# A mixture-of-experts stage in float32: the one-hot gather and combine as two rounded passes, with the routing weights moved to the silu product

## The chip, the cores and the metric

The program runs on one NeuronCore of a Trainium2 chip. The metric is device time in microseconds (us) of one execution. Engines are named as in the profile: PE (TensorE matmul) and PEld (its weight loads), DVE (VectorE), ACT (ScalarE), POOL (GpSimd), and SP, whose queue issues the weight DMAs.

## The reference, cut to what matters

256 tokens of width 1024 pass two blocks. The first has two layers of a mixer, a layer norm, a mixture of experts and a layer norm; the second has dense feed-forward layers and another mixer. The change touches the mixture of experts alone, once in each of the two layers of the first block:

```python
grp_logits = xf @ w_grp + b_grp               # 4 groups, the best one is taken
exp_logits = xf @ w_exp + b_exp               # 8 experts in a group, the best 2 are taken
gate = p_grp[:, None] * softmax(top_l)        # weight of each of a token's 2 experts
...
hdn = silu(xb @ w_gate[e]) * (xb @ w_up[e])   # xb: the tokens of expert e
y = hdn @ w_down[e]
out = zeros.at[tok].add(y * gate_weight)
```

There are 32 experts, each with three float32 matrices of 2 MB (1024 by 512 twice, 512 by 1024 once), so 201 MB are read for each layer. All inputs and outputs are float32.

## The kernel before, in words

**Work.** Experts are taken in 16 pairs of two (`N_PAIRS`); each expert has 64 places (`CAP`), so a pair fills 128 columns. `route_dve` leaves in `k.rank` the place of each token at each expert and in `k.gate_w` its weight. For pair g:

- `select_dve` compares `k.rank` with the numbers 0 to 63 (L1203) into the 0/1 matrix `sel` (two blocks of 128 tokens by 128 places), and multiplies it by `gate_w` (L1212) into `sel_w`.
- `gather_pe` gathers the pair's tokens as a product: for each of 8 slices kk of the width and each of 2 token blocks one float32 matmul with `x_tok[:, tb, kk::8]` as the stationary operand, that is 128 columns whose elements lie 8 words apart, and `sel` as the moving one, 128 wide. It then transposes `sel_w` (L1228). `gather_act` (L1237, L1241) and `gather_dve` (L1249) copy the results out of PSUM to `xg` and `sel_wT`.
- `paired_pe` (L1262) multiplies by gate, up and down: the two experts of the pair use 64 columns of the array each, 512 wide, 16 float32 products for each of the three matrices.
- ACT takes silu (L1326), DVE multiplies by up (L1350) into `h`; PE transposes `h` (L1309), ACT copies it out as `hT` (L1332) for down.
- ACT (L1336) and DVE (L1358) each copy one half of the result `y` out of PSUM. `combine_pe` multiplies the transposed weighted selection by `y`, four float32 products 512 wide, and `combine_dve` adds them to `acc` (L1289).

A line of PE is often that of a helper: L225 is `mm`, which issues the gather, the combine and all projections; the operands tell them apart (gather: `arena,x_tok` 128x128; combine: `arena` 128x512).

**Order.** Each engine runs a list written out by hand. On PE, for pair g: gate(g), up(g), gather(g+1), transposes of h(g), combine(g-1), down(g). After the last pair comes its combine. PSUM has 8 banks of 512 float32; gate uses bank 0, up bank 1, down banks 2 and 3, and all else takes banks 4 to 7 in turn (`B_BANKS`); `Banks.open` waits until the bank's former contents were read.

**Weights.** `Ring` gives each 1 MB chunk of weights a slot. In the expert stages there are 12 slots, which is one pair; SP loads a chunk of pair g+1 when the product that reads the chunk of pair g in its slot has ended (`loads_sp`, L355).

**Rounded operands.** Elsewhere the kernel splits a float32 operand in a rounded high part (float32r, ACT copy, L414) and a low part, the rest (DVE subtract, L421), and sums three rounded products. L1390 is the down product of the dense layers: 4 of them, 22 tiles each, 4 output banks, three products each, 512 wide. `x_tok` is kept in float32; its transposed parts `xT_high` and `xT_low` serve the router and lie idle while the experts run. L449 transposes `x_tok` with the same spaced columns.

Of the kernel before, what the change touches and what calls it, by code (L numbers as in the profile page):

```python
# [6 lines left out]
F32 = mybir.dt.float32  # L7
# [7 lines left out]
P = 128  # L15
# [30 lines left out]
PAIR = 2  # L46
BIG = 1e30
# [1129 lines left out]
def expert_tiles(k):  # L1177
    A = k.arena
    A.restart()
    b = Tiles()  # L1180
    b.sel = [A.take(NB, P) for _ in range(2)]
    b.sel_w = [A.take(NB, P) for _ in range(2)]
    b.sel_wT = [A.take(T) for _ in range(3)]
    b.xg = [A.take(KT, P) for _ in range(2)]
    b.silu, b.h, b.hT = A.take(BANK), A.take(BANK), A.take(FT_E, P)
    b.y = [A.take(D) for _ in range(2)]
    b.spill = [flat(k.mixT[:, :, :]), k.pool_or_distance[:, :]]
    return b


def two_experts(v):
    return v.rearrange("p (a b) -> p a b", a=PAIR)


def select_dve(e, k, X, g):
    S, b, i = X.S, k.experts, g % 2
    e0 = slice(PAIR * g, PAIR * g + PAIR)
    if g >= 2:
        e.wait_ge(*S.product[X.key("gather", g - 2)])
    if g == 0 and X.main:  # L1200
        e.wait_ge(*S.route_step["rank", X.layer])
    for tb in range(NB):
        ins = e.tensor_tensor(two_experts(b.sel[i][:, tb, :]), mid_bcast(k.tab("slot_no"), PAIR), bcast(k.rank[:, tb, e0], CAP), ALU.is_equal)  # L1203
    ins.then_inc(*S.selected.tell(X.key("slots", g)))
    if g == 0 and X.main:
        weigh_dve(e, k, X.layer)
        e.wait_ge(*S.route_step["weights", X.layer])
    e.wait_ge(*S.selected[X.key("slots", g)])
    if g >= 2:
        e.wait_ge(*S.product[X.key("turned_weights", g - 2)])  # L1210
    for tb in range(NB):
        ins = e.tensor_tensor(two_experts(b.sel_w[i][:, tb, :]), two_experts(b.sel[i][:, tb, :]), bcast(k.gate_w[:, tb, e0], CAP), ALU.mult)  # L1212
    ins.then_inc(*S.selected.tell(X.key("weights", g)))


def gather_pe(e, k, X, g):
    S, b, i = X.S, k.experts, g % 2
    for half in range(2):
        view = pairs(X.banks.open(e, B_BANKS, X.key("xg", g, half))[:, :], 4)
        if half == 0:  # L1220
            e.wait_ge(*S.selected[X.key("slots", g)])
        for kk in range(4):
            ins = mm(e, view[:, kk, :], [(k.x_tok[:, tb, (4 * half + kk)::KT], b.sel[i][:, tb, :]) for tb in range(NB)])
        ins.then_inc(*S.product.tell(X.key("gather", g) if half else X.key("gather", g, 0)))
    bank = X.banks.open(e, B_BANKS, X.key("sel_wT", g))
    e.wait_ge(*S.selected[X.key("weights", g)])
    for tb in range(NB):
        ins = e.transpose(bank[:, block(tb)], b.sel_w[i][:, tb, :], k.ident)  # L1228
    ins.then_inc(*S.product.tell(X.key("turned_weights", g)))


def gather_act(e, k, X, g):
    S, b = X.S, k.experts
    if g >= 2:
        e.wait_ge(*S.expert[X.key("up", g - 2, 1)])
    e.wait_ge(*S.product[X.key("gather", g, 0)])
    e.activation(b.xg[g % 2][:, 0:4, :], pairs(X.banks[X.key("xg", g, 0)][:, :], 4), ACT.Copy).then_inc(*S.act_out.tell(X.key("xg", g, 0)))  # L1237
    if g >= 3:
        e.wait_ge(*S.product[X.key("combine", g - 3, 1, 1)])
    e.wait_ge(*S.product[X.key("turned_weights", g)])  # L1240
    e.activation(b.sel_wT[g % 3], X.banks[X.key("sel_wT", g)][:, 0:T], ACT.Copy).then_inc(*S.act_out.tell(X.key("sel_wT", g)))  # L1241


def gather_dve(e, k, X, g):
    S, b = X.S, k.experts
    if g >= 2:
        e.wait_ge(*S.expert[X.key("up", g - 2, 1)])
    e.wait_ge(*S.product[X.key("gather", g)])
    e.tensor_copy(b.xg[g % 2][:, 4:8, :], pairs(X.banks[X.key("xg", g, 1)][:, :], 4)).then_inc(*S.dve_out.tell(X.key("xg", g, 1)))  # L1249
# [17 lines left out]
def combine_pe(e, k, X, g):  # L1267
    S, b, i = X.S, k.experts, g % 2
    for tb in range(NB):
        for n in range(2):  # L1270
            bank = X.banks.open(e, B_BANKS, X.key("add", g, tb, n))
            if tb == 0 and n == 0:
                e.wait_ge(*S.act_out[X.key("sel_wT", g)])
                e.wait_ge(*S.act_out[X.key("y", g, 0)])
                e.wait_ge(*S.dve_out[X.key("y", g, 1)])
            mm(e, bank[:, :], [(b.sel_wT[g % 3][:, block(tb)], b.y[i][:, BANK * n:BANK * n + BANK])]).then_inc(*S.product.tell(X.key("combine", g, tb, n)))
# [15 lines left out]

def experts_pe(e, k, X):
    S, b = X.S, k.experts
    gather_pe(e, k, X, 0)
    for g in range(N_PAIRS):
        i = g % 2
        gate = X.banks.open(e, (0,), X.key("silu", g))
        e.wait_ge(*S.act_out[X.key("xg", g, 0)])
        e.wait_ge(*S.dve_out[X.key("xg", g, 1)])  # L1300
        paired_pe(e, k, X, [gate], "gate", g, KT // 2, b.xg[i])
        up = X.banks.open(e, (1,), X.key("h", g))
        paired_pe(e, k, X, [up], "up", g, KT // 2, b.xg[i])
        if g + 1 < N_PAIRS:
            gather_pe(e, k, X, g + 1)
# [10 lines left out]
    combine_pe(e, k, X, N_PAIRS - 1)  # L1316


def experts_act(e, k, X):
    S, b = X.S, k.experts  # L1320
    gather_act(e, k, X, 0)
    for g in range(N_PAIRS):
# [4 lines left out]
        if g + 1 < N_PAIRS:  # L1327
            gather_act(e, k, X, g + 1)
# [4 lines left out]
        if g >= 2:  # L1333
            e.wait_ge(*S.product[X.key("combine", g - 2, 1, 1)])
        e.wait_ge(*S.expert[X.key("down", g, 1)])
        e.activation(b.y[g % 2][:, 0:BANK], X.banks[X.key("y", g, 0)][:, :], ACT.Copy).then_inc(*S.act_out.tell(X.key("y", g, 0)))  # L1336


def experts_dve(e, k, X):
    S, b = X.S, k.experts  # L1340
    select_dve(e, k, X, 0)
    gather_dve(e, k, X, 0)
    for g in range(N_PAIRS):
        if g + 1 < N_PAIRS:
# [3 lines left out]
        e.wait_ge(*S.act_out[X.key("silu", g)])
        e.wait_ge(*S.expert[X.key("up", g, 1)])
        e.tensor_tensor(b.h, b.silu, X.banks[X.key("h", g)][:, :], ALU.mult).then_inc(*S.dve_out.tell(X.key("h", g)))  # L1350
        if g + 1 < N_PAIRS:
            gather_dve(e, k, X, g + 1)
        if g:
            combine_dve(e, k, X, g - 1)
        if g >= 2:
            e.wait_ge(*S.product[X.key("combine", g - 2, 1, 1)])
        e.wait_ge(*S.expert[X.key("down", g, 1)])
        e.tensor_copy(b.y[g % 2][:, BANK:D], X.banks[X.key("y", g, 1)][:, :]).then_inc(*S.dve_out.tell(X.key("y", g, 1)))  # L1358
# [866 lines left out]
def hgrn_pool(e, k, layer):  # L2225
    S = k.S
    e.wait_ge(*S.act_out["pool", layer, 1])
    if layer:
# [10 lines left out]
           "ffn_high", "ffn_low", "decayed_k", "params_loaded", "wide_loaded", "masks_loaded", "masks_made", "out_stored")  # L2239
# [58 lines left out]
def tiles_and_signals(nc, ctx, A):  # L2298
# [5 lines left out]
    def signal(name):  # L2304
# [11 lines left out]
    k.xh, k.xl = (sb(name, [P, KT, T], F32R) for name in ("xT_high", "xT_low"))  # L2316
    part_slots = [sb(f"w_parts{i}", [P, SLOT]) for i in range(PARTS)]
# [37 lines left out]
    k.arena = Arena(arena, words)  # L2355
# [9 lines left out]
     S.ffn_high, S.ffn_low, S.decayed_k, S.params_loaded, S.wide_loaded, S.masks_loaded, S.masks_made, S.out_stored  # L2365
# [223 lines left out]
def pool_program(e, k, part):  # L2589
    S = k.S  # L2590
    if part == 0:
# [3 lines left out]
        norm_pool(e, k, 0)  # L2595
    elif part == 1:
# [4 lines left out]
        norm_pool(e, k, 2)  # L2601
    else:
# [103 lines left out]
```

## Time and profile before

| | |
|---|---|
| median of 3 runs | 2628.93 us (2626.66 to 2629.95) |
| the profiled execution | 2624.62 us, span 2622.7 us |
| PE busy | 2393.4 us, 91% |
| PEld busy | 1798.1 us, 69% |
| DVE / ACT / POOL busy | 1109.7 / 730.2 / 128.9 us |
| granted TensorE clock, mean | 0.94 |
| read from HBM | 619.51 MB, 237 GB/s over the span |

The expert stages run from about 200 to 730 us and from about 950 to 1480 us. A busy time is the time in which at least one instruction of the engine was under way; matmuls overlap, so the number of them by their mean time is more than the busy time. A float32 matmul appears as two records, each with a weight load of its own; a rounded one appears as one. The clock is in tenths or hundredths of full speed.

### The profile page before, as it was taken

To read this page: it belongs to the slowest core of one execution; us is meant where nothing else is said; L and a number is where in the kernel's file an instruction comes from. 1 tells how busy PE (TensorE), PEld (TensorE's weight loads), DVE (VectorE), ACT (ScalarE), POOL (GpSimd) and SP (SyncE) were. 2 spreads that over 40 slices of the span, in tenths; PEclk is the share of its full clock that TensorE was granted. 3 is DMA by queue.
4 is the path that set the end of the run, shared out by engine and by line. 5 is a ranking of instruction groups with operands and counts; after the bars stand their busy time and mean duration, and the time that the engine had idled before them with its cause. 6 is when DMAs were issued, how large, how long until landed. Compare 5 with 4: busy or idle time off the path is not lost. (4 is left out here: it accounts for less than half of the span.)

```text
span 2622.7 us, 33199 instructions
## 1 busy us (share of the span) xinstructions
PE 2393.4 (91%) x13810; PEld 1798.1 (69%) x13810; DVE 1109.7 (42%) x1650; ACT 730.2 (28%) x1102; POOL 128.9 (5%) x110
## 2 busy tenths in 40 slices
PE   7869999999977879999999799887899899867998
PEld 7866555555466865555555399787899899867997
DVE  4561111111157731111111355657655655567555
ACT  3421000000034210000000144354344344453443
POOL 0010000000011200000000000002000000021000
PEclk9979999999987689999999899998999899888999
DMA  9337999999951169999999755542455455522551
GB/s 293 129 138 291 385 386 385 386 384 386 365 163 65 35 232 381 385 382 388 385 385 385 250 185 177 178 128 65 161 191 182 162 179 179 168 66 89 173 189 65
DMA packets 231554, 622.86 MB, mean 237 GB/s; under 512 B 15457, under 2 KB 166945, under 8 KB 182113
## 3 DMA queue, kind: packets, MB, share of 16 engines
q1 hardware_dynamic: 225952, 604.99, 61.4%
q0 software_dynamic: 3040, 10.78, 1.3%
q10 hardware_dynamic: 2400, 4.83, 0.5%
q8 instruction: 115, 1.88, 0.3%
q14 instruction: 47, 0.38, 0.0%
HBM read 619.51 MB, written 1.05 MB: 237 GB/s over the span
## 5 line engine op out<-in xcount | busy, mean ns | idle before, releaser
L421 DVE TENSOR_TENSOR w_low<-ring,w_high 128x1024 fp32r<-128x1024 f32 x380 | 461.9, 1229 | 395.9 <-ACT w_high L414 395.9
L225 PE MATMUL bank<-xT_high,w_high 128*128 128x256 f32 x1712 | 494.2, 289 | 21.7 <-DVE xT_low L473 13.3
L225 PE MATMUL bank<-xT_low,w_high 128*128 128x256 f32 x1712 | 491.6, 287 | 0.0
L225 PE MATMUL bank<-xT_high,w_low 128*128 128x256 f32 x1712 | 491.2, 287 | 0.0
L414 ACT ACTIVATE w_high<-ring 128x1024 fp32r<-128x1024 f32 x380 | 393.5, 1052 | 344.5 <-PE bank L225 321.6
L1262 PE MATMUL bank<-ring,arena 128*64 128x512 f32 x1792 | 444.7, 592 | 1.4 <-DVE arena L1249 1.4
L225 PEld LDWEIGHTS bank<-xT_high,w_high 128*128 128x128 f32 x1712 | 336.2, 196 | 29.2 <-DVE xT_low L473 14.4
L1262 PEld LDWEIGHTS bank<-ring,arena 128*64 128x64 f32 x1792 | 147.9, 137 | 289.5 <-issue 287.6
L1262 PE MATMUL bank<-w_parts,arena 128*64 128x512 f32 x1024 | 341.6, 595 | 1.7 <-DVE arena L1249 1.7
L225 PEld LDWEIGHTS bank<-xT_low,w_high 128*128 128x128 f32 x1712 | 336.1, 196 | 3.1
L225 PEld LDWEIGHTS bank<-xT_high,w_low 128*128 128x128 f32 x1712 | 335.7, 196 | 0.0
L225 PEld LDWEIGHTS bank<-arena,x_tok 128*128 128x128 f32 x1024 | 247.4, 336 | 27.1 <-issue 24.3
L225 PE MATMUL bank<-arena,x_tok 128*128 128x128 f32 x1024 | 253.4, 407 | 2.5 <-DVE arena L1203 2.5
L1262 PEld LDWEIGHTS bank<-w_parts,arena 128*64 128x64 f32 x1024 | 104.5, 137 | 151.9 <-issue 149.9
L225 PE MATMUL bank<-w_high,xT_high 128*128 128x256 f32 x640 | 191.0, 298 | 3.0 <-DVE xT_low L473 1.5
L1350 DVE TENSOR_TENSOR arena<-arena,bank 128x512 f32<-128x512 f32 x32 | 22.0, 688 | 393.8 <-PE bank L1262 393.8
L225 PE MATMUL bank<-w_low,xT_high 128*128 128x256 f32 x640 | 187.3, 293 | 0.0
L225 PE MATMUL bank<-w_high,xT_low 128*128 128x256 f32 x640 | 186.7, 292 | 0.0
L225 PE MATMUL bank<-arena 128*128 128x512 f32 (+4 forms) x448 | 150.5, 495 | 11.1 <-DVE arena L990 5.2
L1390 PE MATMUL bank<-w_high,hidden_low 128*128 128x512 f32 x352 | 138.7, 394 | 0.0
L1390 PE MATMUL bank<-w_low,hidden_high 128*128 128x512 f32 x352 | 138.4, 393 | 0.0
L1390 PE MATMUL bank<-w_high,hidden_high 128*128 128x512 f32 x352 | 138.2, 393 | 0.0
(254 smaller groups left out, 2385.3 us busy)
## 6 DMA issues: line engine op xcount, KB each, us to landing
ring<-in_moe_w_gate SPq DMA_DIRECT2D x128, 1024.0 KB, 10.4
ring<-in_moe_w_up SPq DMA_DIRECT2D x96, 1024.0 KB, 13.4
w_parts<-in_moe_w_down SPq DMA_DIRECT2D x96, 1024.0 KB, 6.6
ring<-in_ffn_gate SPq DMA_DIRECT2D x44, 1024.0 KB, 6.0
ring<-in_ffn_up SPq DMA_DIRECT2D x44, 1024.0 KB, 5.7
ring<-in_ffn_down SPq DMA_DIRECT2D x44, 1024.0 KB, 5.7
w_parts<-in_moe_w_up SPq DMA_DIRECT2D x32, 1024.0 KB, 15.8
arena<-in_moe_w_down SPq DMA_DIRECT2D x32, 1024.0 KB, 8.7
```

Of the source, the lines that this page charges most:

```text
L225: ins = e.matmul(out, lhs, rhs, start=first and i == 0, stop=last and i == len(parts) - 1)
L414: e.activation(hi, src, ACT.Copy).then_inc(*S.high.tell(key))
L421: e.tensor_tensor(lo, src, hi.bitcast(F32), ALU.subtract).then_inc(*S.low.tell(key))
L1262: ins = e.matmul(tile[r, :], lhs[:, half * per + kk, r], X.ring.view(chunks[j])[:, kk, BANK * n:BANK * n + BANK], start=half == 0 and kk = ...
L1350: e.tensor_tensor(b.h, b.silu, X.banks[X.key("h", g)][:, :], ALU.mult).then_inc(*S.dve_out.tell(X.key("h", g)))
L1390: ins = e.matmul(out, lhs, rhs[:, 0, cols], start=g == 0 and j == 0, stop=g == FT - 1 and j == 2)
```

## The change

- `sel` becomes a rounded tile (0 and 1 are exact in it), one instead of two buffers; `sel_w` and its multiply are gone.
- New `token_parts_act` and `token_parts_pool` split `x_tok` once per layer, ahead of the experts, into `x_tok_high` and `x_tok_low`, which lie in the memory of `xT_high` and `xT_low` with the layout of `x_tok`. ACT copies, POOL subtracts.
- `gather_pe` issues two rounded products, high and low, where it issued one float32 product. Columns of the stationary operand are still 8 words apart, the moving operand still 128 wide.
- `sel` itself is transposed for the combine. The places' weights come from a new small product, `sel` as the stationary operand and two columns of `gate_w` as the moving one, copied to `b.weight` by two small ACT copies; DVE applies them in the product of silu and up, which becomes a `scalar_tensor_tensor`.
- `y` is split: ACT copies both halves rounded to `yh`, DVE subtracts to `yl`; `combine_pe` issues two rounded products for each float32 one. It is called in two parts: token block 0 before the transposes of h, block 1 behind them.
- A pair opens 9 banks of the four in turn instead of 8.
- `scaled_x_act` moves behind `route_act` in ACT's list, and the token split stands where it was.

```diff
+def token_parts_act(e, k, layer):
+    e.wait_ge(*S.used["router", layer])
+    for tb in range(NB):
+        e.activation(k.x_tok_high[:, tb, :], k.x_tok[:, tb, :], ACT.Copy).then_inc(*S.token_high.tell((layer, tb)))
+def token_parts_pool(e, k, layer):
+    for tb in range(NB):
+        e.wait_ge(*S.token_high[layer, tb])
+        e.tensor_tensor(k.x_tok_low[:, tb, :], k.x_tok[:, tb, :], k.x_tok_high[:, tb, :].bitcast(F32), ALU.subtract
+                        ).then_inc(*S.token_low.tell((layer, tb)))
...
+def gather_pe(e, k, X, G):
+    for q in range(2):
+        view = pairs(X.banks.open(e, B_BANKS, X.key("xg", G, q))[:, :], KT // 2)
+        if q == 0:
+            e.wait_ge(*S.selected[X.key("slots", G)])
+            if G == 0 and X.main:
+                e.wait_ge(*S.token_low[X.layer, NB - 1])
+        for i in range(KT // 2):
+            ins = mm(e, view[:, i, :], [(x[:, tb, (KT // 2 * q + i)::KT], b.sel[:, tb, :]) for tb in range(NB) for x in (k.x_tok_high, k.x_tok_low)])
+        ins.then_inc(*S.product.tell(X.key("gather", G, q)))
+    view = pairs(X.banks.open(e, B_BANKS, X.key("selT", G))[:, 0:GATHERED * T], GATHERED)
+    for p in range(GATHERED):
+        for tb in range(NB):
+            ins = e.transpose(view[:, p, block(tb)], b.sel[:, tb, places(p)].bitcast(F32), k.ident)
+    ins.then_inc(*S.product.tell(X.key("selT", G)))
+    bank = X.banks.open(e, B_BANKS, X.key("weights", G))
...
+        ins = mm(e, bank[:, PAIR * p:PAIR * p + PAIR], [(b.sel[:, tb, places(p)].bitcast(F32), k.gate_w[:, tb, e0:e0 + PAIR]) for tb in range(NB)])
...
+def combine_pe(e, k, X, g, tb):
+    turned = b.selT[:, g % KEPT, block(tb)]
+    for n in range(2):
+        bank = X.banks.open(e, B_BANKS, X.key("add", g, tb, n))
+        if tb == 0:
+            e.wait_ge(*S.act_out[X.key("selT", g // GATHERED)])
+            e.wait_ge(*S.dve_out[X.key("y", g, n)])
+        mm(e, bank[:, :], [(turned, b.yh[:, cols]), (turned, b.yl[:, cols])]).then_inc(...)
...
 (experts_pe)
+        if gathered_after(g) is not None:
+            gather_pe(e, k, X, gathered_after(g))
+        if g:
+            combine_pe(e, k, X, g - 1, 0)
         view = pairs(X.banks.open(e, B_BANKS, X.key("hT", g))[:, :], FT_E)
...
         if g:
-            combine_pe(e, k, X, g - 1)
+            combine_pe(e, k, X, g - 1, 1)
...
 (experts_act)
+        for n in range(2):
+            e.activation(b.yh[:, cols], X.banks[X.key("y", g, n)][:, :], ACT.Copy).then_inc(*S.act_out.tell(X.key("y_high", g, n)))
 (experts_dve)
+        e.scalar_tensor_tensor(out=b.h, in0=b.silu, scalar=b.weight[:, i:i + 1], in1=X.banks[X.key("h", g)][:, :], op0=ALU.mult, op1=ALU.mult)
...
+        for n in range(2):
+            e.wait_ge(*S.act_out[X.key("y_high", g, n)])
+            e.tensor_tensor(b.yl[:, cols], X.banks[X.key("y", g, n)][:, :], b.yh[:, cols].bitcast(F32), ALU.subtract)
```

## Rows read from the trace of the kernel before

**Rows 1.** Windows: busy us (count) of PE, PEld, DVE, ACT, POOL; clock, DMA share, GB/s
```profile
449.74:482.48 32.74, 32.74 (x146) 16.60 (x142) 5.71 (x11) 2.77 (x5) 0.00 (x0) 1.00 0.94 383
1100.00:1200.00 100.00, 100.00 (x436) 50.23 (x432) 17.14 (x33) 8.21 (x15) 0.00 (x0) 1.00 0.95 386
```

**Rows 2.** SP's queue, timeline: loads of the next pair's gate weights
```profile
407.27 4.24 SPq L355 DMA_DIRECT2D ring<-in_moe_w_gate  x4
...
440.00 4.24 SPq L355 DMA_DIRECT2D ring<-in_moe_w_gate  x4
```

**Rows 3.** Timeline of one pair in the first expert stage: start us, us, instruction
```profile
417.46 7.73 PEld L225 LDWEIGHTS bank<-arena,x_tok 128*128 128x128 f32 x32 [0.81 <-issue]
...
425.21 0.38 PE L1228 MATMUL bank<-tables,arena 128*128 128x128 f32 x2
...
425.43 0.65 PE L1309 MATMUL bank<-tables,arena 128*128 128x128 f32 x4
425.48 0.69 DVE L1249 COPY arena<-bank 128x512 f32<-128x512 f32 x1 [7.12 <-PE bank L225]
425.69 0.38 ACT L1241 ACTIVATE arena<-bank 128x256 f32<-128x256 f32 x1 [3.46 <-PE bank L1228]
...
425.92 3.60 PE L225 MATMUL bank<-arena 128*128 128x512 f32 x8
426.12 0.60 ACT L1332 ACTIVATE arena<-bank 128x512 f32<-128x512 f32 x1
...
429.44 4.08 PE L1262 MATMUL bank<-w_parts,arena 128*64 128x512 f32 x17
```

**Rows 4.** Timeline of the combine's weight loads in the same pair
```profile
426.78 0.19 PEld L225 LDWEIGHTS bank<-arena 128*128 128x128 f32 x1 [0.24 <-issue]
...
427.21 0.19 PEld L225 LDWEIGHTS bank<-arena 128*128 128x128 f32 x1 [0.24 <-issue]
```

**Rows 5.** Chain that ended last: rounded products 512 wide (L1390)
```profile
1518.21 2.77 PE bank L1390 x12
```

**Rows 6.** Timeline: weight loads with neighbouring columns, and the gather's ahead of stage two
```profile
1767.40 1.76 PEld L1509 LDWEIGHTS bank<-arena,mixT 128*128 128x128 f32 x15
...
950.84 7.72 PEld L225 LDWEIGHTS bank<-arena,x_tok 128*128 128x128 f32 x32 [1.37 <-DVE rank L1134]
```

**Rows 7.** Windows inside the first stage's first gather, columns as in rows 1
```profile
202.00:204.00 2.00, 2.00 (x10) 2.00 (x10) 0.49 (x2) 0.00 (x0) 0.00 (x0) 0.50 0.00 0
```

**Rows 8.** Lines by form, PEld: weight loads of each kind, count, busy us, mean ns
```profile
L225 PEld LDWEIGHTS bank<-arena,x_tok 128*128 128x128 f32 x1024 | 247.4, 336 | 27.1 <-issue 24.3 <-DVE rank L1134 2.7
L1390 PEld LDWEIGHTS bank<-w_high,hidden_high 128*128 128x128 f32 x352 | 66.8, 190 | 11.9
L1262 PEld LDWEIGHTS bank<-ring,arena 128*64 128x64 f32 x1792 | 147.9, 137 | 289.5 <-issue 287.6 <-DVE arena L1249 1.9
```

**Rows 9.** Transposes' loads by source line: min/median/max ns
```profile
L1309 PEld LDWEIGHTS bank<-tables,arena x128: 195/209/218, 231.4 to 1463.8; 128*128 128x128 f32 x128
...
L1228 PEld LDWEIGHTS bank<-tables,arena x64: 141/208/283, 208.3 to 1437.1; 128*128 128x128 f32 x64
```

**Rows 10.** Timeline ahead of the first expert stage
```profile
185.93 2.00 ACT L1091 ACTIVATE acc<-x_tok 128x1024 f32<-128x1024 f32 x2
...
191.39 0.42 DVE L1113 COPY rot_tmp<-bank 36x256 f32<-36x256 f32 x1 [4.63 <-PE bank L225]
...
200.22 0.49 DVE L1203 TENSOR_TENSOR arena<-tables,rank 128x128 f32<-128x128 f32 x2
```

**Rows 11.** Lines by form, POOL: a subtract of 512 columns, mean ns
```profile
L1604 POOL TENSOR_TENSOR mixT<-arena 128x512 f32<-128x512 f32 x32 | 46.7, 1470 | 181.3 <-ACT arena L1588 181.3
```

**Rows 12.** Timeline of the first stage's end
```profile
724.41 0.60 ACT L1336 ACTIVATE arena<-bank 128x512 f32<-128x512 f32 x1 [9.93 <-PE bank L1262]
...
728.98 0.69 DVE L1289 TENSOR_TENSOR acc<-acc,bank 128x512 f32<-128x512 f32 x1 [0.17 <-PE bank L225]
```

**Rows 13.** DMA issues: queue, count, KB each, median us from issue to landing
```profile
ring<-in_moe_w_gate SPq DMA_DIRECT2D x128, 1024.0 KB, 10.4
```

More of the change, by code:

```diff
@@ L46 @@
 PAIR = 2
+GATHERED = 1
+KEPT = 3
 BIG = 1e30
@@ L1180, in expert_tiles @@
     b = Tiles()
[L1181 to L1184, printed above, removed]
+    b.sel = A.take_rounded(NB, GATHERED * P)
+    b.selT = A.take_rounded(KEPT, T)
+    b.xg = A.take(KT, GATHERED * P)
     b.silu, b.h, b.hT = A.take(BANK), A.take(BANK), A.take(FT_E, P)
-    b.y = [A.take(D) for _ in range(2)]
+    b.yh, b.yl = A.take_rounded(D), A.take_rounded(D)
+    b.weight = A.take(KEPT)
@@ L1187, in expert_tiles @@
+    assert A.at <= A.words - SLOT
     b.spill = [flat(k.mixT[:, :, :]), k.pool_or_distance[:, :]]
     return b
[L1191 to L1200, printed above, removed]
+def token_parts_act(e, k, layer):
+    S = k.S
+    e.wait_ge(*S.used["router", layer])
+    for tb in range(NB):
+        e.activation(k.x_tok_high[:, tb, :], k.x_tok[:, tb, :], ACT.Copy).then_inc(*S.token_high.tell((layer, tb)))
@@ new lines, in token_parts_pool, with select_dve @@
+def token_parts_pool(e, k, layer):
+    S = k.S
+    for tb in range(NB):
+        e.wait_ge(*S.token_high[layer, tb])
+        e.tensor_tensor(k.x_tok_low[:, tb, :], k.x_tok[:, tb, :], k.x_tok_high[:, tb, :].bitcast(F32), ALU.subtract
+                        ).then_inc(*S.token_low.tell((layer, tb)))
+def select_dve(e, k, X, G):
+    S, b, n = X.S, k.experts, GATHERED * PAIR
+    experts = slice(n * G, n * G + n)
+    if G:
+        e.wait_ge(*S.product[X.key("weights", G - 1)])
+    elif X.main:
@@ L1211, in select_dve @@
[L1211 to L1229, printed above, removed]
@@ L1232, in gather_act @@
-def gather_act(e, k, X, g):
-    S, b = X.S, k.experts
[L1234 to L1241, printed above, removed]
@@ L1244, in gather_dve, with places @@
-def gather_dve(e, k, X, g):
+        ins = e.tensor_tensor(b.sel[:, tb, :].rearrange("p (a b) -> p a b", a=n), mid_bcast(k.tab("slot_no"), n), bcast(k.rank[:, tb, experts], CAP),
+                              ALU.is_equal)
+    ins.then_inc(*S.selected.tell(X.key("slots", G)))
+def places(p):
+    return slice(p * P, (p + 1) * P)
+def gather_pe(e, k, X, G):
+    S, b = X.S, k.experts
+    for q in range(2):
[13 more added lines that the diff above has]
+    bank = X.banks.open(e, B_BANKS, X.key("weights", G))
+    if G == 0 and X.main:
+        e.wait_ge(*S.route_step["weights", X.layer])
+    for p in range(GATHERED):
+        e0 = PAIR * (GATHERED * G + p)
+        ins = mm(e, bank[:, PAIR * p:PAIR * p + PAIR], [(b.sel[:, tb, places(p)].bitcast(F32), k.gate_w[:, tb, e0:e0 + PAIR]) for tb in range(NB)])
+    ins.then_inc(*S.product.tell(X.key("weights", G)))
@@ new lines, in gather_act @@
+def gather_act(e, k, X, G):
+    S, b = X.S, k.experts
+    at = G % KEPT
+    e.wait_ge(*S.product[X.key("gather", G, 0)])
+    e.activation(b.xg[:, 0:4, :], pairs(X.banks[X.key("xg", G, 0)][:, :], 4), ACT.Copy).then_inc(*S.act_out.tell(X.key("xg", G, 0)))
+    e.wait_ge(*S.product[X.key("selT", G)])
+    e.activation(b.selT[:, at:at + GATHERED, :], pairs(X.banks[X.key("selT", G)][:, 0:GATHERED * T], GATHERED), ACT.Copy).then_inc(*S.act_out.tell(X.key("selT", G)))
+    e.wait_ge(*S.product[X.key("weights", G)])
+    bank = X.banks[X.key("weights", G)]
+    for j in range(PAIR):
+        r = slice(CAP * j, CAP * j + CAP)
+        ins = e.activation(b.weight[r, at:at + GATHERED], bank[r, j:GATHERED * PAIR:PAIR], ACT.Copy)
+    ins.then_inc(*S.act_out.tell(X.key("weights", G)))
@@ L1245, in gather_dve @@
+def gather_dve(e, k, X, G):
     S, b = X.S, k.experts
[L1246 to L1249, printed above, removed]
+    e.wait_ge(*S.product[X.key("gather", G, 1)])
+    e.tensor_copy(b.xg[:, 4:8, :], pairs(X.banks[X.key("xg", G, 1)][:, :], 4)).then_inc(*S.dve_out.tell(X.key("xg", G, 1)))
 def paired_pe(e, k, X, tiles, name, g, per, lhs):
@@ L1264, in paired_pe @@
         ins.then_inc(*X.S.expert.tell(X.key(name, g, half)))
[L1267 to L1276, printed above, removed]
+def combine_pe(e, k, X, g, tb):
+    S, b = X.S, k.experts
+    turned = b.selT[:, g % KEPT, block(tb)]
+    for n in range(2):
+        cols = slice(BANK * n, BANK * n + BANK)
+        bank = X.banks.open(e, B_BANKS, X.key("add", g, tb, n))
+        if tb == 0:
+            e.wait_ge(*S.act_out[X.key("selT", g // GATHERED)])
+            e.wait_ge(*S.dve_out[X.key("y", g, n)])
+        mm(e, bank[:, :], [(turned, b.yh[:, cols]), (turned, b.yl[:, cols])]).then_inc(*S.product.tell(X.key("combine", g, tb, n)))
 def combine_dve(e, k, X, g):
@@ L1290, in combine_dve, with gathered_after @@
                             ).then_inc(*S.dve_out.tell(X.key("add", g, tb, n)))
+def gathered_after(g):
+    G = (g + 1) // GATHERED
+    return G if (g + 1) % GATHERED == 0 and G < N_PAIRS // GATHERED else None
 def experts_pe(e, k, X):
@@ L1315, in experts_pe @@
         paired_pe(e, k, X, tiles, "down", g, FT_E // 2, b.hT)
-    combine_pe(e, k, X, N_PAIRS - 1)
+    for tb in range(NB):
+        combine_pe(e, k, X, N_PAIRS - 1, tb)
 def experts_act(e, k, X):
@@ L1332, in experts_act @@
         e.activation(b.hT, pairs(X.banks[X.key("hT", g)][:, :], FT_E), ACT.Copy).then_inc(*S.act_out.tell(X.key("hT", g)))
-        if g >= 2:
-            e.wait_ge(*S.product[X.key("combine", g - 2, 1, 1)])
+        if g:
+            e.wait_ge(*S.product[X.key("combine", g - 1, 1, 1)])
         e.wait_ge(*S.expert[X.key("down", g, 1)])
-        e.activation(b.y[g % 2][:, 0:BANK], X.banks[X.key("y", g, 0)][:, :], ACT.Copy).then_inc(*S.act_out.tell(X.key("y", g, 0)))
+        for n in range(2):
+            cols = slice(BANK * n, BANK * n + BANK)
+            e.activation(b.yh[:, cols], X.banks[X.key("y", g, n)][:, :], ACT.Copy).then_inc(*S.act_out.tell(X.key("y_high", g, n)))
 def experts_dve(e, k, X):
@@ L1341, in experts_dve @@
     select_dve(e, k, X, 0)
+    if X.main:
+        weigh_dve(e, k, X.layer)
     gather_dve(e, k, X, 0)
@@ L1345, in experts_dve @@
             select_dve(e, k, X, g + 1)
+        e.wait_ge(*S.act_out[X.key("silu", g)])
+        e.wait_ge(*S.act_out[X.key("weights", g // GATHERED)])
+        e.wait_ge(*S.expert[X.key("up", g, 1)])
         if g:
             e.wait_ge(*S.product[X.key("hT", g - 1)])
[L1348 to L1352, printed above, removed]
+        i = g % KEPT
+        e.scalar_tensor_tensor(out=b.h, in0=b.silu, scalar=b.weight[:, i:i + 1], in1=X.banks[X.key("h", g)][:, :], op0=ALU.mult, op1=ALU.mult
+                               ).then_inc(*S.dve_out.tell(X.key("h", g)))
+        if gathered_after(g) is not None:
+            gather_dve(e, k, X, gathered_after(g))
         if g:
             combine_dve(e, k, X, g - 1)
[L1355 to L1358, printed above, removed]
+        if g:
+            e.wait_ge(*S.product[X.key("combine", g - 1, 1, 1)])
+        for n in range(2):
+            cols = slice(BANK * n, BANK * n + BANK)
+            e.wait_ge(*S.act_out[X.key("y_high", g, n)])
+            e.tensor_tensor(b.yl[:, cols], X.banks[X.key("y", g, n)][:, :], b.yh[:, cols].bitcast(F32), ALU.subtract
+                            ).then_inc(*S.dve_out.tell(X.key("y", g, n)))
     combine_dve(e, k, X, N_PAIRS - 1)
@@ L2601, in pool_program @@
         norm_pool(e, k, 2)
+        token_parts_pool(e, k, 1)
     else:
```

48 lines of the change are left out of this document (23 added, 25 removed).

## The prediction

> **What bounds the kernel now.** I read the chain that ended last first. It reaches back only to the start of the second block, so it says nothing of the expert stages; the windows do. Inside both stages PE is busy 100% of the time at full clock, DVE 17%, ACT 8%, and the DMA engines 94% of the time at 383 GB/s [rows 1]. The queue of SP gives the period of a pair: the gate weights are asked for at 407.27 and again at 440.00, that is 32.73 us [rows 2], and 16 pairs in each of two layers are 32 such periods. So two things stand close together: PE, full now, and behind it the DMA. A pair brings 12.58 MB; at 383 GB/s with a share of 0.94 a full share is 408 GB/s, and 12.58 MB at that rate take 30.8 us. PE can be made faster by 1.9 us in a pair before the DMA is full too.
>
> The timeline of one pair says where PE's 32.7 us go [rows 3]: gather 7.75 us (417.46 to the first transpose at 425.21), two transposes of the selection, four of h, the combine from 425.92, down from 429.44; gate, up and down are not touched.
>
> **The gather.** It is bounded by its weight loads: 32 of them fill 7.73 us [rows 3], that is (7.73 - 0.34) / 31 = 0.238 us each, with the last one's own 0.34 taken off [rows 8]. The first gather of a stage, after the quiet of the routing, takes 7.72 us as well in stage two [rows 6], though the granted clock in it is 0.50, that is 1.2 GHz, as stage one shows [rows 7]: what limits the gather does not follow PE's clock. Loads of 128 neighbouring columns with 128-wide float32 products come every (1.76 - 0.19) / 14 = 0.112 us at full clock [rows 6]. So the 8-word step more than doubles the load. After the change there are again 8 slices x 2 blocks x 2 parts = 32 loads with the same step. What does one rounded strided load cost? No row shows one. Rounded loads of neighbouring columns take 190 ns, as the float32 ones do (190), while 64 columns take 137 ns [rows 6, 8]; so a rounded load streams 128 columns no faster than a float32 one: 53 ns for each 64 columns either way. Transposes load faster (141 ns at the least), and those with a 4-word step take 209 [rows 9]: the step multiplies the streaming part by more than two there too. By this likeness the rounded strided load costs 0.238 us and the gather stays at 7.7 us. Lower bound: 0.112, the neighbouring columns' price; it would be 3.6 us. Upper bound: the moving operand in series with the load. Half of a float32 record's 0.107 (the spacing of 0.43 for 512 columns, over four [rows 4]) is 0.053, the whole 0.107, so 0.29 to 0.345 us. I take 0.238, since every kind of load that I can compare agrees in the float32 and the rounded form.
>
> The Trainium skill has a rule on the step, on the page "SBUF — State Buffer", section "SBUF: two separate sides" and its note on cachelines: lines are 16 bytes, and each access that crosses to a new one pays, so that float32 may be spaced up to 4 words free. By it the new gather, at 8 words, pays as the old and the sum below stands, where a price without the step would give the second case below. The trace agrees at 8 words and differs at 4, where the transposes' load grows from 141 to 209 ns [rows 9].
>
> **The combine.** Before: 8 records spaced 0.43 us [rows 4], 3.42 us of PE's stream; the 3.60 of the group includes the last one's latency. After: 4 x 2 = 8 rounded products 512 wide; those of the dense layers come 12 in 2.77 us, 0.231 each [rows 5], so 1.85 us. Saved: 1.57 us. The same kind, width and neighbouring loads, so this price is not in doubt.
>
> **The weights' product.** New: 2 float32 products, 4 records, with two moving columns each. They are load-bound: 4 x 0.112 = 0.45 us [rows 6]; at the most 4 x 0.19 = 0.76, if no load overlaps [rows 8].
>
> **Transposes** keep count and kind. Sum for PE: -1.57 + 0.45 = -1.12 us in a pair, between -0.8 and -1.15.
>
> **New waits on PE.** Let 0 be the end of the gather, 425.21. The selection's transposes end at 0.22, the weights' product at 0.67, block 0 of the combine at 1.59, the transposes of h at 2.05, block 1 at 2.97; then comes down. (1) The second half of block 0 opens the bank of the gather's second half at 1.13; DVE copies that at 425.48 for 0.69 [rows 3], free at 0.96. (2) h's bank was the selection's: ACT's copy ends at 425.69 + 0.38, 0.86, wanted at 1.59. (3) Block 1 opens the weights' bank at 2.05: two ACT copies of about 0.2 us behind the one just named, free at 1.3. (4) Its second bank needs DVE's first add, behind the copy of (1): free at about 2.05, wanted at 2.51. (5) down waits for ACT's copy of h: before, it ended 0.80 us after the transposes left PE's stream (426.72 against 425.92) and 3.4 us of combine covered it [rows 3]. Now only block 1 does, 0.92 us. It is hidden by 0.1 us; I charge 0.04 a pair for what is left of that cover, and 0.8 us would be the price without any. DVE, 17% busy, loses two multiplies and gains two subtracts in place of one copy; ACT gains a copy and two small ones. Both have over 20 us of rest in a pair. h is ready during the gather as before.
>
> **Where a stage begins.** The split of x_tok is new: ACT starts when the router's product ends, about 191.4 [rows 10], two copies of 1.0 us; POOL subtracts 512 columns in 1.47 us [rows 11], so two blocks of 1024 in 5.9 and done at about 198.5. The selection is ready at 200.7 [rows 10]. Cost nothing, with 2.2 us of cover from the routing chain on DVE; if DVE is slowed by POOL beside it, a microsecond or two. scaled_x_act moves behind the routing; its result is wanted a pair later.
>
> **Where a stage ends.** Before: from 724.41 (ACT copies y) to 728.98 + 0.69 = 729.67, 5.3 us [rows 12]. After: the low halves are ready at about 725.8 and 726.5 (two ACT copies of 0.60 and two subtracts of 0.69, one behind the other), block 0 in PE follows, four adds of 0.69 end at about 729.4. Nothing, plus or minus 0.5.
>
> **Sum.** 32 x (1.12 - 0.04) = 34.6 us. The profiled execution took 2624.62 us (span 2622.7), so 2590.0; it lies 4.3 us below the median of the runs, 2628.93, and I carry that over: **2594 us**. With the bounds of the weights' product and the last wait (0.75 to 1.15 a pair, 24 to 37 us) and half of the runs' spread of 3 us: 2590 to 2606 for this case. The DMA then has 32.73 - 1.08 = 31.65 us for what needs 30.8: 97% busy, still not the bound, and a load is asked for almost a pair ahead of its use and lands in 10.4 us [rows 13].
>
> **Rivals.**
> - *Fast gather*: a rounded load reads its columns once and the step costs little. At 0.112 the gather takes 3.6 us, PE's period would be 27.5, and the DMA becomes the bound at 30.8: 15 periods x 1.9 = 29 us in a layer. To this comes the lead: loads are asked for some 29 us before their use (407.27, and about 6.9 us behind down's start at 429.44) and land in 10.4, so PE can run ahead by 19 us before it waits. 48 us in a layer, 96 in all: 2533 us. For it: no row shows a rounded strided load. Against: rounded loads of neighbouring columns are not faster than float32 ones [rows 6, 8]. The Trainium skill gives the ground for it on the page "TensorE: Matmul & The Clock Gate", section "Weight-path perf modes": fast weight load is on for 128 columns when the type is not FP32. The trace's 190 ns for both types does not show it.
> - *Slower*: a rounded product as narrow as 128 does not overlap its load. Place: the 32 products of each gather. At 0.29 us each the gather grows by 1.7 us, and a pair by 0.6: 32 x 0.6 = 19 us, 2648; at 0.345 it is 2.3 us a pair, 2702. It decides from 0.238 + 1.08 / 32 = 0.272 us on. Against: rounded products 512 wide and the float32 ones 128 wide both overlap their loads [rows 5, 6].
> - *No change*: the cover is thinner than I count, and down waits for the copy of h, and block 0 for its banks, about 1 us in a pair. It needs nearly the whole 0.8 us uncovered. 2629.
>
> That the change doesn't do what it says would be a gather in more than one record for each rounded product. Against it: L1390 has 4 layers x 22 tiles x 4 banks = 352 loads for one kind of product [rows 8], one each; the float32 gather has 1024 for 512 products, two each. I give it no chance of its own.
>
> **Chances.** My forecast 0.68, fast gather (or something between the two) 0.19, no change 0.04, slower 0.09. A difference under 0.2% (5.3 us) can't be told from no change here. Faster 0.87, same 0.04, slower 0.09. The range must reach beyond the first case to hold 8 in 10: down to 2531 for the second, up to 2606.
>
> **What would show it.** Period in SP's queue 31.6 us; gather's loads still 32 in 7.7 us with a mean of 0.34; combine 8 products in two groups of 1.85 us together; the weights' loads four at 0.11; PE still at 100% of a window and DMA at 0.97. If the mean load falls below 0.2 us, or DMA shows 1.00 with waits of PE for a ring slot, the second case is true. If PE shows idle time ahead of down, released by ACT's copy of h, step (5) was wrong; ahead of the second combine bank, step (1). If the gather's products are spaced over 0.27 us, I am wrong in sign.

## The result, and the profile after

The changed kernel takes 2680.06 us in the median (2676.26 to 2681.04) against 2628.71 before: 1.9% slower, ratio 1.0193, 95% interval 1.0176 to 1.0211. I had forecast 2594, and gave 0.09 to slower. The profiled execution has a span of 2678.6 us and a mean clock of 0.88, where it was 0.94.

Windows inside both expert stages of the kernel after; columns as in [rows 1], to which they answer:

```profile
400.00:500.00 100.00, 100.00 (x430) 55.98 (x428) 17.63 (x30) 10.78 (x24) 0.00 (x0) 0.85 0.90 368
1200.00:1300.00 100.00, 100.00 (x430) 56.02 (x428) 16.94 (x29) 9.69 (x22) 0.00 (x0) 0.85 0.90 368
```

PE is busy all the time, as before, but the granted clock is 0.85, and the DMA moves less. SP's queue gives the period, answering to [rows 2]:

```profile
427.15 4.24 SPq L357 DMA_DIRECT2D ring<-in_moe_w_gate  x4
...
461.26 4.25 SPq L357 DMA_DIRECT2D ring<-in_moe_w_gate  x4
```

34.11 us in place of 32.73; I had forecast 31.65. The weight loads by form say whether the gather did what I thought (count, busy us, mean ns; they answer to the first of [rows 8]):

```profile
L227 PEld LDWEIGHTS bank<-arena_rounded,xT_low 128*128 128x128 f32 x512 | 172.5, 337 | 0.0
L227 PEld LDWEIGHTS bank<-arena_rounded,xT_high 128*128 128x128 f32 x512 | 171.9, 336 | 27.0 <-issue 24.3 <-DVE rank L1139 2.6
```

1024 loads of 336 ns, as before. The spaced rounded load costs what the spaced float32 one does, and the gather in the timeline lasts from 403.24 to 410.94: 7.70 us. So the loss is not in the gather's own time. Windows over its first part, its second, what follows it, and a stretch of down show where it is:

```profile
403.24:405.90 2.66, 2.66 (x13) 2.66 (x12) 0.75 (x1) 0.00 (x0) 0.00 (x0) 1.00 1.02 422
405.90:410.94 5.04, 5.04 (x22) 5.04 (x23) 0.00 (x0) 0.60 (x1) 0.00 (x0) 0.53 1.01 415
410.94:416.40 5.46, 5.46 (x20) 4.41 (x19) 2.53 (x4) 1.31 (x4) 0.00 (x0) 0.50 1.01 420
417.00:427.00 10.00, 10.00 (x50) 3.37 (x48) 2.06 (x5) 1.09 (x2) 0.00 (x0) 1.00 0.64 243
```

Within the gather, at about 406.2, the granted clock falls from 1.00 to 0.50 (2.4 to 1.2 GHz), and it comes back only at about 416.4, just ahead of down. PE and its weight loads had been busy without a gap since the gather began. The gather itself takes no longer at the lower clock. All that stands behind it does; its timeline answers to [rows 3]:

```profile
410.98 0.65 PE L1246 MATMUL bank<-tables,arena_rounded 128*128 128x128 f32 x2
411.21 0.98 PEld L227 LDWEIGHTS bank<-gate_w,arena_rounded 128*128 128x128 f32 x4
...
412.14 2.05 PE L227 MATMUL bank<-arena_rounded 128*128 128x512 f32 x4
...
413.99 1.05 PE L1345 MATMUL bank<-tables,arena 128*128 128x128 f32 x4
...
414.70 1.96 PE L227 MATMUL bank<-arena_rounded 128*128 128x512 f32 x4
...
415.08 0.60 ACT L1369 ACTIVATE arena<-bank 128x512 f32<-128x512 f32 x1 [2.43 <-PE bank L1345]
```

From the gather's end to down (416.58) it is 5.64 us, where I had counted 2.97 and the kernel before took 4.23. The combine's eight rounded products cost about 0.43 us each instead of 0.231 (DVE's adds, one for every two products, start at 413.38 and 414.23), and the four loads of the weights' product fill 0.98 us where I had 0.45.

The second loss is ahead of the stage. DVE and POOL in the timeline of the routing:

```profile
197.17 4.64 POOL L1209 TENSOR_TENSOR xT_low<-x_tok,xT_high 128x1024 fp32r<-128x1024 f32 x2 [7.75 <-ACT xT_high L1202]
197.20 0.15 DVE L1106 TENSOR_REDUCE group_max<-group_logits 128x2 f32<-128x8 f32 x1
197.38 2.16 DVE L1108 TENSOR_TENSOR group_hot<-group_logits,group_max 128x8 f32<-128x8 f32 x1
199.57 2.27 DVE L1110 TENSOR_TENSOR group_hot<-group_hot,tables 128x8 f32<-128x8 f32 x1
201.88 0.16 DVE L1112 TENSOR_REDUCE place<-group_hot 128x2 f32<-128x8 f32 x1
...
209.02 0.49 DVE L1222 TENSOR_TENSOR arena_rounded<-tables,rank 128x128 fp32r<-128x128 f32 x2
```

Two DVE steps on 8 columns take 2.16 and 2.27 us, one for each of POOL's subtracts; before, steps of this kind took 0.17. From the copy of the logits (196.10) to the selection (209.02) it is 12.92 us, against 200.22 - 191.39 = 8.83 [rows 10].

The parts, from the two profiles: selection to last add 529.45 and 529.8 us before, 550.2 and 551.0 after (+20.7, +21.2); routing +4.1 and +4.2. Together 50.2, and the medians differ by 51.4. Fifteen gathers in each layer stand inside the stage, and 15 x 1.38 = 20.7, but that is a round account: the period is 33.6 us in the second and third pair and creeps up to 34.13. The spans of the two profiled executions differ by 55.9, 5.7 more than the parts; 4.7 of this lie ahead of the first routing, where both do the same work. The start of the routing lies anywhere from 191.4 to 197.0 in the profiles of all ten kernels, so I put nothing of it down to the change.

### The profile page after: what moved, and what is told of

Its sections match the earlier page's. It is cut to its first block and busy times, and to the rows that moved or that the text cites. A ratio compares the mean times of both kernels' runs of the same rounds, so it can differ in the third digit from the quotient of the medians.

```text
span 2678.6 us, 33419 instructions
## 1 busy us (share of the span) xinstructions
PE 2445.8 (91%) x13938; PEld 1872.5 (70%) x13938; DVE 1121.8 (42%) x1618; ACT 761.3 (28%) x1202; POOL 138.3 (5%) x114
## 5 line engine op out<-in xcount | busy, mean ns | idle before, releaser
L227 PE MATMUL bank<-arena_rounded,xT_high 128*128 128x128 f32 x512 | 220.2, 430 | 2.4 <-DVE rank L1139 2.4
L227 PE MATMUL bank<-arena_rounded,xT_low 128*128 128x128 f32 x512 | 218.6, 427 | 0.0
L227 PEld LDWEIGHTS bank<-arena_rounded,xT_high 128*128 128x128 f32 x512 | 171.9, 336 | 27.0 <-issue 24.3
L1393 DVE SCALAR_TENSOR_TENSOR arena<-arena,bank 128x512 f32<-128x512 f32 x32 | 23.9, 748 | 375.8 <-PE bank L1288 375.8
L227 PEld LDWEIGHTS bank<-arena_rounded,xT_low 128*128 128x128 f32 x512 | 172.5, 337 | 0.0
L1404 DVE TENSOR_TENSOR arena_rounded<-bank,arena_rounded 128x512 fp32r<-128x512 f32 x64 | 41.2, 686 | 236.9 <-ACT arena_rounded L1375 236.9
```

What stands on the lines that cost most here:

```text
L227: ins = e.matmul(out, lhs, rhs, start=first and i == 0, stop=last and i == len(parts) - 1)
L1393: e.scalar_tensor_tensor(out=b.h, in0=b.silu, scalar=b.weight[:, i:i + 1], in1=X.banks[X.key("h", g)][:, :], op0=ALU.mult, op1=ALU.mult).t ...
L1404: e.tensor_tensor(b.yl[:, cols], X.banks[X.key("y", g, n)][:, :], b.yh[:, cols].bitcast(F32), ALU.subtract).then_inc(*S.dve_out.tell(X.key ...
```

## The experiments

**Clock or combine?** The first run leaves every load and result of the change in place and only gives PE more columns to move:

```diff
-            ins = mm(e, view[:, i, :], [(x[:, tb, (KT // 2 * q + i)::KT], b.sel[:, tb, :]) for tb in range(NB) for x in (k.x_tok_high, k.x_tok_low)])
+            parts = [(x[:, tb, (KT // 2 * q + i)::KT], b.sel[:, tb, :]) for tb in range(NB) for x in (k.x_tok_high, k.x_tok_low)]
+            out = view[:, i, :]
+            if i < KT // 2 - 1:
+                out, parts = view[:, i:i + 2, :], [(lhs, mid_bcast(rhs, 2)) for lhs, rhs in parts]
+            ins = mm(e, out, parts)
```

> The changed kernel, but in 3 of 4 slices of the gather the moving operand is the selection twice, 256 columns instead of 128; the second 128 results are overwritten by the next slice. Same loads, same results, more moving columns. Theory A (the clock falls because the rounded gather moves so few columns for each load, and everything behind it runs at 1.2 GHz): clock 1.0 in the gather and behind it, the gather still 7.7 us, a pair 31.6 us instead of 34.1, the kernel about 2602 us. Theory B (the rounded combine in two parts is itself slower than its neighbours in the dense layers, or waits for banks; the clock only goes with it): nothing changes or the gather grows, 2680 us or more.

Measured: 2603.83 us, ratio to before (2627.10 beside it) 0.992 (0.9903 to 0.9936). Windows:

```profile
400.00:500.00 100.00, 100.00 (x466) 52.91 (x464) 17.10 (x30) 10.91 (x25) 0.00 (x0) 1.00 0.96 392
```

Timeline of SP's queue and of what follows one gather on PE:

```profile
408.24 4.24 SPq L357 DMA_DIRECT2D ring<-in_moe_w_gate  x4
...
426.20 0.40 PE L1250 MATMUL bank<-tables,arena_rounded 128*128 128x128 f32 x2
...
426.81 1.17 PE L227 MATMUL bank<-arena_rounded 128*128 128x512 f32 x4
...
427.81 0.63 PE L1349 MATMUL bank<-tables,arena 128*128 128x128 f32 x4
...
428.20 1.17 PE L227 MATMUL bank<-arena_rounded 128*128 128x512 f32 x4
...
439.86 4.24 SPq L357 DMA_DIRECT2D ring<-in_moe_w_gate  x4
```

The clock stays at 1.00, a pair takes 31.62 us, and the same combine products take 1.17 us for four. More work in PE made the kernel 76 us faster than the change. Theory B falls: nothing in the combine or its banks was altered. Of theory A this shows that the rounded gather's form brings the clock down and that the clock costs the time; that the number of columns for each load is what counts is the nearest reading, not a measured rule.

**The change with the gather of before:**

```diff
-            ins = mm(e, view[:, i, :], [(x[:, tb, (KT // 2 * q + i)::KT], b.sel[:, tb, :]) for tb in range(NB) for x in (k.x_tok_high, k.x_tok_low)])
+            ins = mm(e, view[:, i, :], [(k.x_tok[:, tb, (KT // 2 * q + i)::KT], b.sel[:, tb, :].bitcast(F32)) for tb in range(NB)])
...
-        token_parts_act(e, k, 0)
...
-        token_parts_pool(e, k, 0)
```

> The changed kernel with the gather of before: one float32 product from x_tok, spaced columns; no split of x_tok at all. Combine in two rounded parts, weights' product and all else stay. Theory A: the clock stays at 2.4 GHz, a pair takes 31.6 us, routing takes 8.8 us as before, the kernel 2594 us, my forecast for the whole. Theory B (the combine's new form or its bank waits cost the time): a pair stays above 33 us, 2640 us or more.

Measured: 2591.43 us, ratio 0.9869 (0.9853 to 0.9886). The gather and what follows it in the timeline:

```profile
413.99 7.73 PEld L227 LDWEIGHTS bank<-arena_rounded,x_tok 128*128 128x128 f32 x32 [0.81 <-issue]
...
421.75 0.38 PE L1244 MATMUL bank<-tables,arena_rounded 128*128 128x128 f32 x2
...
424.84 4.08 PE L1286 MATMUL bank<-w_parts,arena 128*64 128x512 f32 x17
...
435.40 4.24 SPq L357 DMA_DIRECT2D ring<-in_moe_w_gate  x4
...
467.00 4.24 SPq L357 DMA_DIRECT2D ring<-in_moe_w_gate  x4
```

3.09 us from the gather to down (I had 2.97), 31.60 us for a pair (31.65). In sum the combine, the weights' product, the new bank order and the thinner cover of h's copy cost what the prediction said. The change also leaves `xg` and `y` one buffer each where they had two, which the list of the change does not name; this run has that too, and loses nothing by it.

**The rounded gather alone**, in the kernel before (low part on DVE):

```diff
+    token_parts_dve(e, k, layer)
...
-            ins = mm(e, view[:, kk, :], [(k.x_tok[:, tb, (4 * half + kk)::KT], b.sel[i][:, tb, :]) for tb in range(NB)])
+            ins = mm(e, view[:, kk, :], [(x[:, tb, (4 * half + kk)::KT], b.sel[i][:, tb, :]) for tb in range(NB) for x in (k.x_tok_high, k.x_tok_low)])
```

> The kernel before with the rounded spaced gather alone (low part of x_tok on DVE); combine in float32, weights by multiply, as before. Theory A: the clock falls in each gather and is at 1.2 GHz for about 5 us behind it, so that most of the float32 combine runs at 0.86 us a record: a pair 35.2 us, the kernel about 2710 us. Theory B (the gather's loads cost the same, the loss is in the combine): a pair 32.7 us, 2630 us.

Measured: 2685.02 us in a single run. Theory B falls: the loss is there with the old combine, so the gather alone makes it, and the two stages are 27.6 and 27.4 us longer than before. Theory A's size is missed: 35.2 us holds for the second pair alone, and a later one takes 34.17, +1.44 and not +2.5. SP's queue, and windows over the clock's low stretch in the second pair and in a later one:

```profile
254.57 4.24 SPq L355 DMA_DIRECT2D ring<-in_moe_w_gate  x4
...
289.82 4.95 SPq L355 DMA_DIRECT2D ring<-in_moe_w_gate  x4
...
427.40 4.24 SPq L355 DMA_DIRECT2D ring<-in_moe_w_gate  x4
...
461.57 4.24 SPq L355 DMA_DIRECT2D ring<-in_moe_w_gate  x4
```

```profile
267.43:277.67 10.24, 10.24 (x33) 8.05 (x34) 1.60 (x3) 1.58 (x3) 0.00 (x0) 0.50 1.02 420
407.38:414.20 6.82, 6.82 (x26) 5.79 (x26) 0.69 (x1) 1.58 (x3) 0.00 (x0) 0.50 1.01 420
```

The loads of the float32 combine in the later pair show what the shorter stretch gives back:

```profile
413.27 0.34 PEld L225 LDWEIGHTS bank<-arena 128*128 128x128 f32 x1 [0.52 <-issue]
414.12 0.23 PEld L225 LDWEIGHTS bank<-arena 128*128 128x128 f32 x1 [0.52 <-issue]
...
414.60 0.19 PEld L225 LDWEIGHTS bank<-arena 128*128 128x128 f32 x1 [0.24 <-issue]
```

Their spacing goes from 0.85 to 0.48 at about 414.1: the clock came back inside this combine, some 2 us earlier than behind the rounded one. I had carried over the time of its return from another sequence of work, and that does not carry. It does not even carry from pair to pair of one kernel: the same work saw a low stretch of 10.2 us in the second pair and of 6.8 in the later ones. Nor is it the combine alone that sets the time: this kernel comes down from 35.25 us a pair to 34.13 by the end of the stage, the changed one creeps up from 33.63 to the same 34.13, although its combine needs 1.57 us less at full clock. What leads both there stays open.

**The low part on DVE instead of POOL:**

```diff
     e.tensor_tensor(R.hot, R.oh1, R.oh2, ALU.add).then_inc(*step.tell(("chosen", layer)))
+    token_parts_dve(e, k, layer)
...
-        token_parts_pool(e, k, 0)
```

> The changed kernel with the low part of x_tok subtracted on DVE, behind the step that makes the chosen_hot rows, instead of on POOL. Theory A (POOL's subtract holds up DVE's steps of the routing, 2.16 and 2.27 us in place of 0.17): routing from the logits' copy to the selection falls from 12.9 to about 9.2 us in each layer, the kernel to about 2673 us. Rival (ACT's split in front of the routing's exponentials is what delays it): routing stays at 12.9 us or grows by DVE's own 2.6 us; 2680 to 2685 us.

Measured: 2671.87 us in a single run. The steps are short again, and the subtract lies in DVE's wait for PE's counting of places:

```profile
192.92 0.42 DVE L1118 COPY rot_tmp<-bank 36x256 f32<-36x256 f32 x1 [5.63 <-PE bank L227]
...
194.20 0.17 DVE L1108 TENSOR_TENSOR group_hot<-group_logits,group_max 128x8 f32<-128x8 f32 x1
...
198.59 2.35 DVE L1210 TENSOR_TENSOR xT_low<-x_tok,xT_high 128x1024 fp32r<-128x1024 f32 x2
...
201.75 0.50 DVE L1223 TENSOR_TENSOR arena_rounded<-tables,rank 128x128 fp32r<-128x128 f32 x2
```

Routing takes 8.83 us, as before, in both layers, and 2 x 4.1 us are back. ACT's split still stands ahead of the routing's exponentials here, so the rival falls.

**The step of the columns.** The expensive term of the gather is untouched by all this: 0.24 us for a load. ACT can write the columns of a slice side by side once per layer:

```diff
+def by_slice(k, tb):
+    return k.x_tok[:, tb, :].rearrange("p (c k) -> p k c", k=KT)
...
+        e.activation(k.x_tok_near[:, tb, :, :], by_slice(k, tb), ACT.Copy)
...
-            ins = mm(e, view[:, kk, :], [(k.x_tok[:, tb, (4 * half + kk)::KT], b.sel[i][:, tb, :]) for tb in range(NB)])
+            ins = mm(e, view[:, kk, :], [(k.x_tok_near[:, tb, 4 * half + kk, :], b.sel[i][:, tb, :]) for tb in range(NB)])
```

This is an edit of the kernel before, all in float32, and nothing else of the change:

> The kernel before with one edit: ACT copies x_tok once per layer, in float32, so that the 128 columns of a slice are neighbours, and the gather's stationary operand is read from that copy. Theory A (the 8-word step is the price of the gather's load, 0.24 us against 0.112): the gather falls from 7.7 to about 3.7 us, PE needs 28.7 us for a pair, and the DMA becomes the bound at about 30.5 us: about 2540 us. Rival (the load costs what it costs by its type, the step is not the cause): the gather stays 7.7 us, 2627 us.

Measured: 2529.96 us, ratio 0.9627 (0.9611 to 0.9643). Windows of the stages:

```profile
400.00:500.00 100.00, 97.74 (x481) 41.77 (x482) 19.43 (x39) 8.91 (x16) 0.00 (x0) 1.00 1.01 420
1200.00:1300.00 100.00, 95.75 (x470) 41.05 (x468) 17.15 (x33) 8.91 (x16) 0.00 (x0) 1.00 1.01 420
```

Timeline of a pair: PE's wait for a chunk of weights, and the gather's loads:

```profile
507.03 0.61 PE L1275 MATMUL bank<-ring,arena 128*64 128x512 f32 x1 [0.98 <-DMA w_parts<-in_moe_w_up]
...
510.61 3.65 PEld L225 LDWEIGHTS bank<-arena,x_tok_near 128*128 128x128 f32 x32 [0.81 <-issue]
```

32 loads in 3.65 us, 0.112 each. The DMA is now full (1.01, 420 GB/s), and PE waits for it. Up to about 440 us the period is PE's own, 28.65 us (gate weights asked for at 410.57 and 439.22); then the lead that the loads had is used up, and it is 29.9 (469.35 to 499.23). 12.58 MB at 420 GB/s are 30.0 us a pair, less than the 30.8 that I had from the share of 0.94.

The same copy in the changed kernel with a float32 gather:

> As the run with the float32 gather in the changed kernel (2591 us), but the gather reads a float32 copy of x_tok with neighbouring columns. Theory A: gather 3.7 us, PE would need 27.6 us for a pair, but the DMA is the bound at about 30.5 us: the same time as the kernel before with that copy, about 2540 us. If PE were still the bound in some way, about 2480 us.

Measured: 2528.29 us, ratio 0.9628 (0.9612 to 0.9644). The same time, with PE busy 92.89 us from 400 to 500 instead of 97.74, and 92.55 from 1200 to 1300 instead of 95.75: what the rounded combine saves goes into waiting for weights. And the rounded gather with neighbouring columns, low part on DVE, then on POOL:

```diff
-            ins = mm(e, view[:, i, :], [(x[:, tb, (KT // 2 * q + i)::KT], b.sel[:, tb, :]) for tb in range(NB) for x in (k.x_tok_high, k.x_tok_low)])
+            ins = mm(e, view[:, i, :], [(x[:, tb, KT // 2 * q + i, :], b.sel[:, tb, :]) for tb in range(NB) for x in (k.x_tok_high, k.x_tok_low)])
```

> The changed kernel with rounded gather, its two parts laid out with neighbouring columns, and the low part subtracted on DVE. If a rounded load follows the step as a float32 one does, the gather takes 32 x 0.12 = 3.9 us and its moving columns fill 0.053 of 0.12 us, against 0.053 of 0.24 in the changed kernel and 0.107 of 0.24 in the one before, where the clock stayed up: then the clock stays at 2.4 GHz, and the DMA is the bound, about 2540 us. Rival (rounded loads are not helped by the layout): 2672 us as with the spaced ones.

> As the run before in this list, but the low part on POOL as in the changed kernel: it shows what POOL costs in the routing when x_tok is read with the step by POOL: about 8 us more over two layers than on DVE, or more if POOL's subtract itself gets slower than 2.3 us for 1024 columns.

Measured: 2538.86 us, ratio 0.9663 (0.9647 to 0.9679), with DVE, and 2548.72 in a single run with POOL. Windows of the first over a gather and over 100 us of a stage:

```profile
515.36:519.00 3.64, 3.64 (x35) 3.64 (x33) 0.75 (x1) 0.60 (x1) 0.00 (x0) 1.00 1.02 423
...
400.00:500.00 100.00, 92.95 (x482) 43.00 (x482) 19.14 (x34) 11.83 (x27) 0.00 (x0) 1.00 1.01 420
```

The gather's rounded products come every 0.11 us and the clock stays at 1.00: rounded and 128 wide is not enough to bring it down. But this gather is both denser and shorter. It ends after 3.64 us, while in the changed kernel the clock fell 2.7 to 5.8 us after a gather's start; so the run does not say which of the two keeps the clock up. The first is slower than the float32 copy in the same kernel by 10.6 us. 2.6 of them lie in the routing (10.13 us from the logits' copy to the selection in the first layer, against 8.82), where the two subtracts take 3.94 us on DVE in place of 2.35; they now read x_tok with the step. The stages are 2.5 and 2.2 us longer (477.2 and 478.4), and 2.4 lie behind the second; these I did not follow. With POOL the subtracts take 5.65 us and the routing 14.05, that is 3.9 us more in a layer than with DVE, or about the 8 in all that I expected.

## Why the prediction was wrong, by its own steps

- *The gather stays at 7.7 us, since the rounded strided load costs 0.238.* Right: 7.70 us, 336 ns a load. The likeness of the float32 and the rounded loads [rows 8] held, with the step and without it.
- *The combine: 0.231 us a product, "this price is not in doubt".* **This is the step that failed**, and with it the weights' product and "transposes keep count and kind". All three prices came from rows at full clock, and I carried them behind a gather that I had just made into something else without asking what clock it would leave. They held to 0.05 us a pair where the clock stayed up (the run with the old gather), and measured 5.64 us instead of 2.97 where it did not. In the changed kernel the combine's products cost 0.43 us each at 1.2 GHz instead of 0.231. The size: 34.11 - 31.65 us for each of 30 gathers inside the stages, 74 of the 86 us between forecast and result; by whole stages, against the run with the old gather, 79.
- *What would show it:* the list gives one sign of a slower kernel, products of the gather spaced over 0.27 us. They were not, and the kernel was slower all the same; the granted clock stands on no line of the list.
- The sign was in my reach. I noted that the gather "does not follow PE's clock" and wrote down the moving time of a rounded product, 0.053 us for a load of 0.238, but asked only whether the two overlap. With the same loads the change halves what moves through the array. The Trainium skill, on its page "TensorE: Matmul & The Clock Gate", section "HAM oscillation", tells of PE falling to its lower clock when it waits; here it fell with no wait at all, weight loads busy through the whole gather, and it stayed up when more columns were moved for the same loads.
- *Slower, my rival:* wrong mechanism. Its products would be spaced by more than 0.272 us; they are spaced 0.24.
- *Fast gather, my rival:* its time, 2533 us, is near what the neighbouring columns gave (2530 and 2528), and its mechanism is what they show: DMA the bound, once the loads' lead is used up. That the number fits so well is in part luck. In the float32 kernel the stages became 52.0 and 51.2 us shorter and not 48, and some 9 us of this were lost outside them, 2.8 between the stages and 4.9 behind the second. Its condition was wrong: the type does not remove the step's price, the layout does.
- *The step in the transposes, from 141 to 209 ns [rows 9]:* that compares the least of one kind with the median of the other, and both medians are about 208; the selection's transposes stand right behind the spaced loads. The run with neighbouring columns has the clean pair: 142 ns in the mean for the selection's (L1241), 207 for h's with its 4-word step (L1322). The reading holds, on other rows.
- *New waits on PE:* right in sum, 3.09 for 2.97 us; the profile names none of the five as a wait of PE.
- *Where a stage begins: nothing, or a microsecond or two if DVE is slowed by POOL.* Mis-sized: 4.1 and 4.2 us, 8.3 of the 86. POOL was done at 201.8, 4.64 us for both blocks and so faster than the 5.9 that I had; what I left out is what DVE has to do meanwhile. The Trainium skill says it, on the page "SBUF — State Buffer", section "Who interferes with whom": a DVE instruction with two SBUF inputs and a POOL instruction that reads SBUF lock each other out. The trace agrees: L1108 and L1110 with two inputs take 2.16 and 2.27 us, the reduction L1106, with one input, starts under POOL's subtract as well and takes 0.15.
- *Where a stage ends: nothing, plus or minus 0.5.* Right as far as it can be read: from ACT's copies of y in the last pair to the last add it took 729.67 - 724.41 = 5.3 us before and 759.21 - 754.46 = 4.8 us after, in the first stage.

Shown: that the clock's fall comes with the spaced rounded gather and goes with wider moving operands, with the old gather and with neighbouring columns; and that without the fall the rest of the change costs what was forecast. Open: what in the gather the chip goes by, whether with neighbouring columns it is the density or the shorter time that keeps the clock up, and what sets the times at which the clock falls and returns.

## What to carry to other kernels

Before a product is made cheaper, look at what bounds it: here the weight load's 8-word step. The rounding left it in place; one strided copy per layer removed it and saved 97 us. A passage of PE that is all loads and few moved columns can lower the clock for everything behind it, so price the steps behind a changed one at both clocks, and read the granted clock beside the busy share. And when a second engine is given a large elementwise step, ask which short steps of the critical chain run at that time.

## What the runs showed of the hardware that was not expected

- The granted clock fell to 1.2 GHz with PE at 100% busy and no wait, in the middle of a 7.7 us run of weight loads with 128 rounded moving columns each; 256 columns in three of four of them kept it at 2.4 GHz in the same 7.7 us. In steady pairs the low stretch was 10.2 us long in the changed kernel and 6.8 us in the one with the old combine, and both came to the same 34.13 us a pair.
- A spaced load (8 words) takes 0.24 us at either clock, float32 or rounded; with neighbours 0.112 at full clock, both.
- Two DVE steps on 8 columns with two inputs take 2.16 and 2.27 us instead of 0.17 while POOL subtracts; a reduction with one input takes its 0.15.
- The expert weights' DMA, in 1 MB transfers, moves 420 GB/s over 100 us in the runs in which PE waits for it, against 383 to 386 before.
- ACT's strided read of 1024 columns takes 1.99 us instead of 1.00, DVE's subtract 1.97 instead of 1.18.
